# Attention halves stored apart and added at the output projection, inverse roots spread by transposes, and a new order of the attention's steps

## The chip, the core and the metric

The kernel runs on one core of a Trainium2 chip. A core has TensorE (matrix products), VectorE, ScalarE, GpSimd and SyncE, which here only issues DMAs. Each works off its own queue of instructions in order and waits on semaphores for the others. In the profile they are PE (PEld for its weight loads), DVE, ACT, POOL and SP. The metric is the device time of one execution in microseconds (us), as the median of several runs.

## The reference

Two groups of tokens, 1024 and 512, go through one encoder layer with a model width of 1024. All is f32. Cut to what matters:

```python
def _encoder_layer(x, mem, ...):
    h = _rmsnorm(x, norm_mix_g)
    dq, dk, dv, gq, gk, gv = jnp.split(h @ w_in, SPLITS, axis=-1)
    ...                                            # partial rope on dq, dk
    d_out = _diff_attention(dq, dk, dv, lam)       # 4 heads of 128, p0 - lam * p1
    d_out = _rmsnorm(d_out, diff_subln_g) * (1.0 - lambda_init)
    ...                                            # head norm and axial rope on gq, gk
    g_out = _gqa_attention(gq, gk, gv)             # 8 query heads of 64, 2 key/value heads
    x = x + jnp.concatenate([d_out, g_out], axis=-1) @ w_out
    h, m = _rmsnorm(x, norm_xattn_g), _rmsnorm(mem, norm_mem_g)
    ...                                            # cross attention, 4 heads of 256, 256 memory tokens
    h = _rmsnorm(x, norm_ffn_g)
    u = h @ w_up                                   # 1024 x 5632, then a convolution of width 3
    ...
    x = x + (jax.nn.silu(a) * b) @ w_down
    return x                                       # a last _rmsnorm follows
```

## The kernel before

Every f32 operand of a product is split into an upper and a lower part (`hi`, `lo`), and each product is made of three: hi x hi, lo x hi, hi x lo. Tokens are taken in 12 tiles of 128 (8 of the first group, 4 of the second).

The first part of the program (`trunk_phase`, until about 866 us) computes keys and values of the memory (`kv`, L838), the input projection (`proj`, L865), and the attention. The attention goes over 72 pairs of query tiles, numbered by `no`: pairs 0 to 23 belong to the four differential heads, 24 to 71 to the two groups of four query heads. For each pair TensorE computes scores (L895 to L905), ScalarE their exponentials (L1044), TensorE turns the probabilities (`turn`, L918), ScalarE and VectorE split them (`hi` L1053, `lo` L1184), and TensorE sums them into one accumulator `t_acc` in PSUM, of 128 rows by 256 queries (`mix`, L939). For a grouped-query head, rows 0 to 63 and rows 64 to 127 of the accumulator are two partial sums over different keys.

Out of the accumulator:

- Differential head: ScalarE copies it to `mixed` (`out`, L1060) and squares it. TensorE sums the squares (`sumsq`, L959), VectorE takes the mean, GpSimd the inverse root of 2 x 128 numbers (`sub_rstd`, L795) and two diagonal matrices with them (L798). TensorE multiplies these with a matrix of ones (`spread`, L966), by which each inverse root stands in all rows of its query's column, and VectorE multiplies (`finish`, L1197). SyncE stores 128 rows to `mix_scratch` in DRAM (L642).
- Grouped-query head: ScalarE copies rows 64 to 127 to `sq` (L1070), VectorE adds them to rows 0 to 63 (`merge`, L1203) once the buffer's store of two pairs before has landed, and SyncE stores 64 rows (L646). The next pair's first product into the accumulator waits for the merge (L939).

In the last part of the attention SyncE also loads w_out in eight parts (`out_load`, L654), which GpSimd splits (`out_split`, L703), and the first four tiles of `mix_scratch` (`mix_load`, L663), 512 KB each, which ScalarE and VectorE split (L1075 and the line `mix_lo`). The first products of the output projection are made at its end (`first_acc`, L951).

The second part (`rest_phase`) begins with the output projection: tile after tile in four parts (`acc`, L2202), VectorE adds x (`y`, L2744), ScalarE squares (L2437), VectorE takes the mean (L2748), GpSimd the inverse root (`rstd`, L1976), VectorE scales (`scale`, L2754), and TensorE turns the normed tile (`norm_turn`, L2217). Tiles 4 to 11 are loaded from `mix_scratch` (L1724) and split (`m_hi` L2431, `m_lo` L2738). GpSimd splits the query weights of the cross attention (L1986, L1989), and VectorE sums blocks of w_up (L2790). Cross attention and the convolutional network follow until 2366 us.

The order on each engine comes from planners. `plan` gives every step of the attention an engine, a due time, a duration and what it has to come after. `SHIFT` is a table of numbers that are added to the due times by kind of step and stage, and `PATIENCE` says for each engine how long it would rather wait for a step that is due sooner:

```python
    def put(self, engine, due, takes, kind, what, *after):
        rank = due + self.shift.get(stage_of(kind, what), {}).get(kind, 0.0) if self.shift else due
...
                    key = (max(r - free[e] - self.patience[e], 0.0), due)
                    if choice is None or key < choice[0]:
                        choice = (key, max(r, free[e]), kind)
```

`rest_plan` does the same for the second part, without such a table.

## Time and profile before

| | |
|---|---|
| time, median of 3 runs | 2368.79 us (2365.97 to 2370.07) |
| profiled execution | 2368.59 us, its span in the profile 2366.8 us |
| mean granted TensorE clock | 0.995 of full speed |
| TensorE busy | 2313.6 us, 98% |
| VectorE, GpSimd, ScalarE busy | 1780.4, 1321.2, 1147.3 us |
| DMA | 368.96 MB, mean 156 GB/s |

The busy time of an engine counts its instructions but not its semaphores and branches. A line of the timeline has the start, the duration and the instruction with output<-inputs; in brackets stands how long the engine was idle before it and what ended that. A count "x6" with a duration joins a run of equal instructions. The granted clock is the share of full speed that TensorE was given in a stretch. "DMA share" is the mean busy share of the 16 DMA engines; it can come out over 1 where packets lie over each other.

### The profile page before, as it was taken

The numbers are of one execution on the slowest core, as the hardware profiler recorded it, in microseconds if no ns is written. First come the engines' busy times: TensorE is split into PE (matmuls) and PEld (weight loads), VectorE is DVE, ScalarE is ACT, GpSimd is POOL, SyncE is SP. The second block draws the span as 40 slices with busy tenths as digits, with TensorE's granted clock in tenths as the row PEclk, the third lists the DMA queues.
The fourth block names the chain that finished last, engine by engine and source line by source line (L and its number), as shares of the span: only waits on it lengthen the run. The fifth ranks groups of instructions, "written<-read, shape, count | busy, mean of one in ns | idle before, by whom it ended". The sixth has DMA issues, their size and how long they took to land.

```text
span 2366.8 us, 34336 instructions
## 1 busy us (share of the span) xinstructions
PE 2313.6 (98%) x12096; PEld 1982.9 (84%) x12096; DVE 1780.4 (75%) x2644; ACT 1147.3 (48%) x2288; POOL 1321.2 (56%) x1522
## 2 busy tenths in 40 slices
PE   8999999999999999999999999999999999999998
PEld 7998998889998978888878888878877888888886
DVE  5447777889888967676643379988768888888888
ACT  4446665656677852123322245544444444444444
POOL 3453644688878612063150067767656666666663
PEclk9999999999999999999999999999999999999999
DMA  8853434432222049888863344333353333333332
GB/s 355 337 213 130 161 132 163 172 109 90 96 81 84 13 153 331 288 298 289 301 238 133 107 169 134 116 120 129 121 192 94 100 94 96 100 94 97 100 94 111
DMA packets 163209, 368.96 MB, mean 156 GB/s; under 512 B 16864, under 2 KB 52064, under 8 KB 152544
## 3 DMA queue, kind: packets, MB, share of 16 engines
q1 hardware_dynamic: 163040, 366.77, 45.3%
q8 instruction: 98, 1.61, 0.3%
q14 instruction: 71, 0.58, 0.1%
HBM read 284.92 MB, written 81.79 MB: 155 GB/s over the span
## 4 chain that ended last, share of the span: by engine, by line
PE 79%; DVE 8%; POOL 4%; DMA 4%; issue 3%; ACT 1%; SPq 1%; POOLq 0%; DVEq 0%; ACTq 0%
PE r_bank L2296 28%; PE r_bank L2202 10%; PE t_proj L865 9%; PE r_bank L2170 8%; PE r_bank L2235 4%; PE t_acc L939 4%; PE t_turn L918 3%; PE t_scores L838 2%; PE t_scores L895 1%; PE r_bank L2283 1%; PE r_bank L2254 1%; PE t_scores L899 1%; PE t_scores L904 1%; PE t_scores L905 1%; PE t_acc L865 1%
## 5 line engine op out<-in xcount | busy, mean ns | idle before, releaser
L865 PE MATMUL t_proj<-t_w_hi,t_hbuf 128*128 128x384 f32 x1056 | 306.2, 344 | 0.0
L2943 DVE TENSOR_TENSOR r_x_p<-r_bank,r_x_p 128x512 f32<-128x512 f32 x280 | 182.8, 682 | 48.0 <-PE r_bank L2296 47.0
L1164 DVE TENSOR_REDUCE t_max_neg<-t_scores 128x1 f32<-128x1024 f32 (+1 forms) x192 | 195.6, 1037 | 20.2 <-PE t_scores L899 17.2
L1044 ACT ACTIVATE t_prob<-t_scores,t_max_neg 128x1024 f32<-128x1024 f32 (+1 forms) x192 | 187.4, 979 | 38.6 <-DVE t_max_neg L1164 30.9
L865 PEld LDWEIGHTS t_proj<-t_w_hi,t_hbuf 128*128 128x128 f32 x1056 | 193.9, 188 | 7.3 <-issue 5.8
L1184 DVE TENSOR_TENSOR t_pt_lo<-t_turn,t_pt_hi 128x512 fp32r<-128x512 f32 x240 | 163.4, 687 | 39.9 <-ACT t_pt_hi L1053 36.7
L1053 ACT CAST t_pt_hi<-t_turn 128x512 fp32r<-128x512 f32 x240 | 139.9, 587 | 106.2 <-PE t_turn L918 84.5
L2797 DVE SCALAR_TENSOR_TENSOR r_conv<-r_rows,r_taps,r_conv 128x511 f32<-128x511 f32 (+3 forms) x134 | 157.1, 1173 | 30.2 <-ACT r_conv L2592 27.9
L865 PE MATMUL t_proj<-t_w_lo,t_hbuf 128*128 128x384 f32 x528 | 177.4, 336 | 0.0
L1976 POOL TENSOR_TENSOR r_stat<-r_stat,minus_half 128x1 f32<-128x1 f32 x24 | 16.1, 669 | 268.4 <-DVE r_stat L2748 268.4
L2044 POOL TENSOR_TENSOR r_s_lo<-r_s_raw,r_s_hi 128x512 fp32r<-128x512 f32 x87 | 128.2, 1479 | 61.7 <-ACT r_s_hi L2490 61.7
L2071 POOL TENSOR_TENSOR r_wd_lo<-r_wd_raw,r_wd_hi 128x512 fp32r<-128x512 f32 x72 | 110.7, 1538 | 79.7 <-ACT r_wd_hi L2495 79.3
L2044 POOL TENSOR_TENSOR r_w_lo<-r_w_raw,r_w_hi 128x512 fp32r<-128x512 f32 x67 | 114.8, 1715 | 72.1 <-ACT r_w_hi L2490 72.1
L918 PE MATMUL t_turn<-ident,t_prob 128*128 128x128 f32 x960 | 142.3, 274 | 3.7 <-DVE t_qk L1159 1.9
L939 PE MATMUL t_acc<-t_pt_hi,t_v_hi 128*128 128x256 f32 x480 | 139.7, 308 | 6.3 <-DVE t_mixed L1203 4.0
L2170 PE MATMUL r_bank<-r_hs_hi,r_w_hi 128*128 128x512 f32 x352 | 137.8, 391 | 4.1 <-DVE r_s_conv L2797 4.1
L2027 POOL TENSOR_TENSOR r_sd_lo<-r_sd_raw,r_sd_hi 128x512 fp32r<-128x512 f32 x74 | 109.0, 1477 | 58.8 <-ACT r_sd_hi L2504 58.6
L2170 PE MATMUL r_bank<-r_hs_hi,r_w_lo 128*128 128x512 f32 x352 | 137.5, 391 | 0.0
L2170 PE MATMUL r_bank<-r_hs_lo,r_w_hi 128*128 128x512 f32 x352 | 137.4, 390 | 0.0
L939 PE MATMUL t_acc<-t_pt_lo,t_v_hi 128*128 128x256 f32 x480 | 127.6, 282 | 0.0
L918 PEld LDWEIGHTS t_turn<-ident,t_prob 128*128 128x128 f32 x960 | 112.2, 141 | 18.1 <-issue 6.4
L2022 POOL TENSOR_TENSOR r_w_lo<-r_stage,r_w_hi 128x1024 fp32r<-128x1024 f32 x42 | 103.7, 2468 | 34.0 <-ACT r_w_hi L2485 34.0
(350 smaller groups left out, 7371.5 us busy)
## 6 DMA issues: line engine op xcount, KB each, us to landing
t_hbuf<-split_x SPq DMA_DIRECT2D x60, 1024.0 KB, 4.8
block_sums<-r_block SPq DMA_DIRECT2D x128, 256.0 KB, 3.2
r_block<-in_w_up_units SPq DMA_DIRECT2D x88, 256.0 KB, 4.7
r_stage<-in_w_up_units SPq DMA_DIRECT2D x44, 512.0 KB, 3.5
r_s_raw<-block_sums SPq DMA_DIRECT2D x87, 256.0 KB, 2.6
r_w_raw<-in_w_up_units SPq DMA_DIRECT2D x66, 256.0 KB, 2.6
split_x<-t_hbuf SPq DMA_DIRECT2D x12, 1024.0 KB, 8.7
r_block<-in_w_down SPq DMA_DIRECT2D x40, 256.0 KB, 4.5
```

What stands on the lines that cost most here:

```text
L865: ins = nc.tensor.matmul(proj_bank(i), l, r[:, k, :], start=(k == 0 and j == 0), stop=(k == KT - 1 and j == 2))
L918: ins = nc.tensor.transpose(ps_t[:, slot, kk * 2 * P + qt * P:kk * 2 * P + (qt + 1) * P], prob[:, n % PSLOTS, keys], ident[:, :])
L939: ins = nc.tensor.matmul(ps_o[:, 0:2 * P], l, r, start=(c == 0 and kk == 0 and j == 0), stop=(c == p.chunks - 1 and kk == 1 and j == len(t ...
L1044: nc.scalar.activation(prob[:, n % PSLOTS, 0:p.keys], ps_s[:, n % 2, 0:p.keys], ACT.Exp, bias=max_neg[:, n % COLS:n % COLS + 1], accum_out ...
L1164: nc.vector.tensor_reduce(max_neg[:, n % COLS:n % COLS + 1], ps_s[:, n % 2, 0:p.keys], AX.X, ALU.max, negate=True).then_inc(max_done, 1)
L1184: nc.vector.tensor_tensor(pt_lo[:, n % 2, :], ps_t[:, slot, :], f32(pt_hi[:, n % 2, :]), ALU.subtract).then_inc(ptlo_done, 1)
L2044: nc.gpsimd.tensor_tensor(wop_lo[slot][:, :], wop_raw[slot][:, :], f32(wop_hi[slot][:, :]), ALU.subtract).then_inc(op_ready, 1)
L2170: ins = nc.tensor.matmul(one_bank(s), l, r, start=(k == 0 and j == 0), stop=(k == KT - 1 and j == 2))
L2202: ins = nc.tensor.matmul(acc(t)[:, cols], l[:, k, :], r[:, cols], start=(k == 0 and j == 0), stop=(k == KT - 1 and j == 2), skip_group_che ...
L2296: ins = nc.tensor.matmul(out, l, r, start=(first and j == 0), stop=(last and j == 2), skip_group_check=onto)
L2797: return nc.vector.scalar_tensor_tensor(out, src, tap_of(j, s, i), out, ALU.mult, ALU.add)
L2943: nc.vector.tensor_tensor(x_p[:, t, cols], down_bank(q), x_p[:, t, cols], ALU.add).then_inc(p_add, 1)
```

## The change

There are three parts, and nothing else in what is computed changes.

**Halves stored apart.** `mix_scratch` has 512 more rows. For a grouped-query pair ScalarE now copies all 128 rows of the accumulator to `mixed`, as for a differential one, after the store of two pairs before has landed. SyncE stores both halves, 128 KB, to two places. `merge` is gone from VectorE. The next pair's first product waits for the copy. Where a tile is loaded for the output projection, a second DMA of 256 KB brings the other halves of the grouped-query heads into the upper-part buffer (`h_hi`), and GpSimd adds them in, 128 x 4 x 128 elements, before ScalarE's split: `mix_add` for tiles 0 to 3, `m_add` for tiles 4 to 11.

**Inverse roots.** The diagonal matrices and the product with ones are replaced by two transposes of a column of inverse roots that is read 128 times.

**Order.** `SHIFT` and `PATIENCE` have new numbers, a few due times and conditions follow the parts above, and the new GpSimd steps enter both plans. At the start all four loads of memory now come before the first load of its weights, and VectorE splits all eight parts of the memory (L1087) ahead of the first weights (L1093), where it split two, then the weights, then six. In the second part TensorE's second and fourth `norm_turn` stand one part of the projection later.

```diff
-PATIENCE = {"PE": 0.0, "DVE": 0.289, "ACT": 0.314, "POOL": 0.203, "SP": 0.0}
+PATIENCE = {"PE": 0.0, "DVE": 0.0, "ACT": 0.565, "POOL": 0.516, "SP": 0.0}
 SHIFT = {
-    "": {"axial_load": -234.355, "first_acc": 105.798, "h_load": -442.544, "key_out": -603.419, "key_store": -87.738,
+    "": {"axial_load": -1070.3, "first_acc": 971.055, "h_load": -128.363, "key_out": 128.746, "key_store": 588.333,
...
@@ plan
-            put("POOL", b + 2.0, 1.4, "sub_rstd", (p,), ("sub_mean", (p,)))
-            put("PE", b + 3.6, 0.5, "spread", (p,), ("sub_rstd", (p,)))
-            put("DVE", b + 4.4, 0.45, "finish", (p,), ("spread", (p,)))
+            put("POOL", b + 2.0, 0.7, "sub_rstd", (p,), ("sub_mean", (p,)), ("spread", (pairs[p.no - 2],)) if p.no >= 2 else None)
+            put("PE", b + 2.9, 0.22, "spread", (p,), ("sub_rstd", (p,)))
+            put("DVE", b + 3.6, 0.45, "finish", (p,), ("spread", (p,)))
...
-            put("ACT", b, 0.38, "out", (p,), ("mix", (p, p.chunks - 1)), merged, ("spread", (prev,)) if prev.diff else None)
-            put("DVE", b + 0.4, 0.42, "merge", (p,), ("out", (p,)), ("store", (pairs[p.no - 2],)))
-            put("SP", b + 1.0, 0.07, "store", (p,), ("merge", (p,)))
+            put("ACT", b, 0.38, "out", (p,), ("mix", (p, p.chunks - 1)), ("store", (pairs[p.no - 2],)))
+            put("SP", b + 0.5, 0.13, "store", (p,), ("out", (p,)))
...
-        put("ACT", pairs[-3].start + 4 * t, 1.06, "mix_hi", (t,), ("mix_load", (t,)))
+        put("POOL", pairs[-3].start + 4 * t - 1.5, 1.1, "mix_add", (t,), ("mix_load", (t,)))
+        put("ACT", pairs[-3].start + 4 * t, 1.06, "mix_hi", (t,), ("mix_add", (t,)))
@@ trunk_phase
-                        sp.wait_ge(merged, p.no - n_diff + 1)
-                        sp.dma_start(head_rows(p), mixed[0:HD, p.no % 2, :]).then_inc(mixed_stored[p.no % 2], 16)
+                        sp.wait_ge(copied, p.no + 1)
+                        sp.dma_start(head_rows(p), mixed[:, p.no % 2, :]).then_inc(mixed_stored[p.no % 2], 16)
...
+                    sp.dma_start(h_raw[0][:, :, cols], turned_mix[:, 0:KT, cols]).then_inc(tile_loaded[t % 2], 16)
+                    sp.dma_start(f32(h_hi[0][:, HK:KT, cols]), turned_mix[:, KT:KT + HK, cols]).then_inc(tile_loaded[t % 2], 16)
...
+                elif kind == "mix_add":
+                    t, = what
+                    pool.wait_ge(tile_loaded[t % 2], 32 * (t // 2 + 1))
+                    cols = slice(t * P, (t + 1) * P)
+                    raw = h_raw[0][:, HK:KT, cols]
+                    nc.gpsimd.tensor_tensor(raw, raw, f32(h_hi[0][:, HK:KT, cols]), ALU.add).then_inc(tile_added, 1)
...
-                    pool.wait_ge(sub_rstd_done, p.no + 1)
-                    for qt in range(2):
-                        nc.gpsimd.tensor_scalar(sq[:, qt * P:(qt + 1) * P], ident[:, :], sub_r[:, p.no % 2, qt:qt + 1], 1.0,
-                                                ALU.mult, ALU.mult).then_inc(sub_diag_done, 1)
...
-                    nc.tensor.matmul(ps_t[:, slot, 0:2 * P], ones[:, :], sq[:, :], start=True, stop=True).then_inc(spread_done, 1)
+                    for qt in range(2):
+                        column = sub_r[:, p.no % 2, qt:qt + 1].to_broadcast([P, P])
+                        ins = nc.tensor.transpose(ps_t[:, slot, qt * P:(qt + 1) * P], column, ident[:, :])
+                    ins.then_inc(spread_done, 1)
...
-                        nc.scalar.copy(sq[0:HD, :], ps_o[HD:P, 0:2 * P]).then_inc(copied, 1)
...
-                elif kind == "merge":
-                    p, = what
-                    dve.wait_ge(*stored_before(p))
-                    dve.wait_ge(copied, p.no + 1)
-                    nc.vector.tensor_tensor(mixed[0:HD, p.no % 2, :], ps_o[0:HD, 0:2 * P], sq[0:HD, :], ALU.add).then_inc(merged, 1)
@@ rest_plan
-            put("ACT", b - 4, 1.06, "m_hi", (t,), ("m_load", (t,)))
+            if not xo:
+                put("POOL", b - 6, 1.1, "m_add", (t,), ("m_load", (t,)))
+            put("ACT", b - 4, 1.06, "m_hi", (t,), ("m_load", (t,)) if xo else ("m_add", (t,)))
@@ rest_phase
+                    if t < NT:
+                        lows = mix_view[:, KT:KT + HK, t * P:(t + 1) * P]
+                        sp.dma_start(f32(m_tiles(t)[0][:, HK:KT, :]), lows).then_inc(m_loaded[n % 4], 16)
...
+                if kind == "m_add":
+                    t, = what
+                    n = t - EARLY
+                    pool.wait_ge(m_loaded[n % 4], m_count(n))
+                    hi, _, raw = m_tiles(t)
+                    nc.gpsimd.tensor_tensor(raw[:, HK:KT, :], raw[:, HK:KT, :], f32(hi[:, HK:KT, :]), ALU.add).then_inc(m_added, 1)
```

Line numbers in the rows of the changed kernel below are its own: L646 is L649 there, L654 is L657, L663 is L667 and L668, L1976 is L1989, L1986 and L1989 are L1999 and L2002.

SyncE's queue around the loads of w_out (`wo_raw`), before, in the second group of query heads:

```order
152 L646 DMA mix_scratch<-t_mixed 64x256 x8
153 L654 DMA wo_raw_75<-in_w_out 128x1024
154 L654 DMA wo_raw_76<-in_w_out 128x1024
155 L654 DMA wo_raw_77<-in_w_out 128x1024
156 L654 DMA wo_raw_78<-in_w_out 128x1024
157 L654 DMA wo_raw_79<-in_w_out 128x1024
158 L654 DMA wo_raw_80<-in_w_out 128x1024
159 L654 DMA wo_raw_81<-in_w_out 128x1024
160 L654 DMA wo_raw_82<-in_w_out 128x1024
161 L646 DMA mix_scratch<-t_mixed 64x256 x17
```

The same place now:

```order
142 L649 DMA mix_scratch<-t_mixed 2x64x256 x8
143 L657 DMA wo_raw_75<-in_w_out 128x1024
144 L657 DMA wo_raw_76<-in_w_out 128x1024
145 L657 DMA wo_raw_77<-in_w_out 128x1024
146 L649 DMA mix_scratch<-t_mixed 2x64x256
147 L657 DMA wo_raw_78<-in_w_out 128x1024
148 L657 DMA wo_raw_79<-in_w_out 128x1024
149 L657 DMA wo_raw_80<-in_w_out 128x1024
150 L657 DMA wo_raw_81<-in_w_out 128x1024
151 L657 DMA wo_raw_82<-in_w_out 128x1024
152 L649 DMA mix_scratch<-t_mixed 2x64x256 x16
```

One store of a pair has moved in after the third of the eight loads.

SyncE's queue at the end of the attention, where the first four tiles are loaded (`h_raw`, and now `h_hi` for the other halves), before:

```order
161 L646 DMA mix_scratch<-t_mixed 64x256 x17
162 L663 DMA h_raw_89<-mix_scratch 128x8x128 x3
163 L646 DMA mix_scratch<-t_mixed 64x256
164 L663 DMA h_raw_89<-mix_scratch 128x8x128
165 L646 DMA mix_scratch<-t_mixed 64x256 x6
```

And now, behind the same store (of pair 63):

```order
153 L667 DMA h_raw_89<-mix_scratch 128x8x128
154 L668 DMA h_hi_83<-mix_scratch 128x4x128
155 L667 DMA h_raw_89<-mix_scratch 128x8x128
156 L668 DMA h_hi_83<-mix_scratch 128x4x128
157 L667 DMA h_raw_89<-mix_scratch 128x8x128
158 L668 DMA h_hi_83<-mix_scratch 128x4x128
159 L667 DMA h_raw_89<-mix_scratch 128x8x128
160 L668 DMA h_hi_83<-mix_scratch 128x4x128
161 L649 DMA mix_scratch<-t_mixed 2x64x256 x7
```

The store of pair 64 stood behind three loads and now stands behind four tiles of two loads each.

GpSimd's queue at the start of the output projection (`r_stat` rows are inverse roots, `r_wxq` the splits of w_xq), before:

```order
720 L1976 TENSOR_TENSOR r_stat<-r_stat,minus_half 128x1 x2
721 L1986 TENSOR_SCALAR r_wxq_hi_14172<-r_wxq_raw_14176 128x512
722 L1989 TENSOR_TENSOR r_wxq_lo_14174<-r_wxq_raw_14176,r_wxq_hi_14172 128x512
...
728 L1989 TENSOR_TENSOR r_wxq_lo_14174<-r_wxq_raw_14176,r_wxq_hi_14172 128x512
729 L1976 TENSOR_TENSOR r_stat<-r_stat,minus_half 128x1 x10
```

And now:

```order
721 L1989 TENSOR_TENSOR r_stat<-r_stat,minus_half 128x1
722 L1983 TENSOR_TENSOR h_raw_90<-h_raw_90,h_hi_84 128x4x128
723 L1989 TENSOR_TENSOR r_stat<-r_stat,minus_half 128x1
724 L1999 TENSOR_SCALAR r_wxq_hi_14014<-r_wxq_raw_14018 128x512
...
733 L2002 TENSOR_TENSOR r_wxq_lo_14016<-r_wxq_raw_14018,r_wxq_hi_14014 128x512
734 L1983 TENSOR_TENSOR h_raw_90<-h_raw_90,h_hi_84 128x4x128
735 L1989 TENSOR_TENSOR r_stat<-r_stat,minus_half 128x1
736 L1983 TENSOR_TENSOR h_raw_91<-h_raw_91,h_hi_85 128x4x128 x4
737 L1989 TENSOR_TENSOR r_stat<-r_stat,minus_half 128x1 x9
```

The first addition stands ahead of the second inverse root, two more (rows 726 and 731, left out) among the four splits, the fourth ahead of the third root, and four ahead of the fourth.

## Rows read from the trace of the kernel before

**Rows 1.** The page's part 1: busy time, share and instructions of each engine.

```profile
PE 2313.6 (98%) x12096; PEld 1982.9 (84%) x12096; DVE 1780.4 (75%) x2644; ACT 1147.3 (48%) x2288; POOL 1321.2 (56%) x1522
```

**Rows 2.** TensorE's waits, whole span: line <- releaser: us, times, longest.

```profile
PE t_scores L838 <- DVE t_xkv_lo L1093: 8.7, 2, 8.5
...
PE t_acc L939 <- DVE t_mixed L1203: 4.0, 3, 1.9
PE r_bank L2217 <- DVE r_normed L2754: 3.7, 1, 3.7
...
PE t_turn L918 <- DVE t_qk L1159: 1.9, 3, 1.0
```

**Rows 3.** Windows: length, PE, PEld, DVE, ACT, POOL busy, granted clock, DMA share, GB/s.

```profile
700.00:750.00 50.00, 47.22 (x310) 42.28 (x310) 45.20 (x96) 39.54 (x90) 42.36 (x65) 1.00 0.23 68
757.60:761.00 3.40, 3.40 (x15) 3.16 (x14) 2.49 (x6) 1.58 (x3) 2.84 (x4) 0.50 0.09 19
834.80:866.00 31.20, 28.55 (x181) 24.12 (x180) 24.76 (x48) 22.11 (x48) 8.85 (x11) 1.00 0.33 93
880.00:898.00 18.00, 14.29 (x63) 11.54 (x62) 16.11 (x17) 7.44 (x9) 8.88 (x7) 0.91 1.11 341
```

**Rows 4.** Timeline of TensorE, a spread at 352.9 and two transposes at 231.2.

```profile
231.22 0.42 PE L878 MATMUL t_turn<-ident,t_nat 128*128 128x128 f32 x2
231.39 0.42 PE L865 MATMUL t_proj<-t_w_hi,t_hbuf 128*128 128x384 f32 x1
...
352.91 0.59 PE L966 MATMUL t_turn<-t_sq,t_ones 128*128 128x256 f32 x2
353.15 0.47 PE L939 MATMUL t_acc<-t_pt_hi,t_v_hi 128*128 128x256 f32 x1
```

**Rows 5.** Groups of instructions, 0 to 880 us: busy, mean ns | idle before.

```profile
L703 POOL TENSOR_TENSOR wo_lo<-wo_raw,wo_hi 128x512 fp32r<-128x512 f32 x16 | 20.6, 1289 | 1.3
...
L1203 DVE TENSOR_TENSOR t_mixed<-t_acc,t_sq 64x256 f32<-64x256 f32 x48 | 19.7, 410 | 8.7 <-ACT t_sq L1070 5.0 <-DMA mix_scratch<-t_mixed 3.5
```

**Rows 6.** Timeline at the w_out loads, SyncE and VectorE.

```profile
738.44 14.04 SPq L654 DMA_DIRECT2D wo_raw<-in_w_out  x8
...
756.75 0.42 DVE L1203 TENSOR_TENSOR t_mixed<-t_acc,t_sq 64x256 f32<-64x256 f32 x1 [2.31 <-DMA mix_scratch<-t_mixed]
```

**Rows 7.** Timeline of the start, ScalarE, VectorE and TensorE.

```profile
7.78 2.02 DVE L1093 TENSOR_TENSOR t_xkv_lo<-t_xkv_raw,t_xkv_hi 128x256 fp32r<-128x256 f32 x4
8.17 3.96 ACT L978 ACTIVATE t_mem_hi<-t_mem_raw,t_gain_cols 128x512 fp32r<-128x512 f32 x6 [1.29 <-DMA t_mem_raw<-in_mem_turned]
...
9.72 5.62 DVE L1087 SCALAR_TENSOR_TENSOR t_mem_lo<-t_mem_raw,t_gain_cols,t_mem_hi 128x512 fp32r<-128x512 f32 x6
...
27.85 0.33 PE L865 MATMUL t_proj<-t_w_hi,t_hbuf 128*128 128x384 f32 x1
```

**Rows 8.** Timeline at the end of the attention, SyncE and TensorE.

```profile
837.80 4.48 SPq L663 DMA_DIRECT2D h_raw<-mix_scratch  x3
...
847.34 0.36 PE L939 MATMUL t_acc<-t_pt_hi,t_v_hi 128*128 128x256 f32 x1 [1.14 <-DVE t_mixed L1203]
```

**Rows 9.** Timeline at the start of the output projection, four engines.

```profile
887.07 1.04 ACT L2431 CAST h_hi<-h_raw 128x1024 fp32r<-128x1024 f32 x1 [1.04 <-DMA h_raw<-mix_scratch]
...
889.62 1.09 PE L2217 MATMUL r_bank<-ident,r_normed 128*128 128x128 f32 x8 [3.71 <-DVE r_normed L2754]
...
890.73 2.13 POOL L1989 TENSOR_TENSOR r_wxq_lo<-r_wxq_raw,r_wxq_hi 128x512 fp32r<-128x512 f32 x1
...
900.71 1.29 POOL L1989 TENSOR_TENSOR r_wxq_lo<-r_wxq_raw,r_wxq_hi 128x512 fp32r<-128x512 f32 x1
...
903.23 0.55 POOL L1976 TENSOR_TENSOR r_stat<-r_stat,minus_half 128x1 f32<-128x1 f32 x1 [1.23 <-DVE r_stat L2748]
903.82 1.28 DVE L2754 SCALAR_TENSOR_TENSOR r_normed<-r_x_mo,r_stat,r_gain 128x1024 f32<-128x1024 f32 x1 [0.66 <-POOL r_stat L1976]
...
905.79 1.03 PE L2217 MATMUL r_bank<-ident,r_normed 128*128 128x128 f32 x8
```

107 lines of the change are left out of this document (55 added, 52 removed).

## The prediction

> **What bounds the kernel now.** I read the page's busy shares first, then TensorE's waits by line, then windows of single stretches with their granted clock, then the timeline at the four places that the change touches. TensorE is busy 98% of a span of 2366.8 us; VectorE has 75%, GpSimd 56% [rows 1]. So only two things count: TensorE's own work, and the few places where it runs dry. Those are short: all its waits for the merged halves make 4.0 us in three, those at the first memory projection 8.7, the one for a normed tile at the output projection 3.7 [rows 2]. A wait costs more than itself where the clock falls: after the longest wait for a merge the granted clock was 0.50 for 3.4 us, at which 3.4 us hold 1.7 us of work [rows 3] (its second line). VectorE is the engine nearest behind in the second half of the attention, 45.2 us of 50 [rows 3] (its first line). The profiled execution took 2368.59 us, 1.8 more than its span, and is 0.2 below the median of the three runs. A measurement of this kernel can tell about 0.2% from no change, that is 4.7 us.
>
> **1. Root spread by transposes.** Before, one product with the matrix of ones stands in two records, and the next instruction starts 0.24 us after the first of them (352.91 to 353.15). Two transposes of 128x128 let the next start after 0.17 (231.22 to 231.39) [rows 4]. There are 24 pairs of differential heads, so 24 x -0.07 = -1.7 us, in a stretch in which TensorE is hardly ever idle: I take **-2**. GpSimd loses 48 instructions that it makes the diagonal with, on no path that waits. The Trainium skill speaks against this edit ("TensorE: Matmul & The Clock Gate", Part 4: PE-mode transpose): a 128x128 transpose takes some 275 ns in a kernel, most of it the access of SBUF. The records do last 0.27 (0.42 for two, the second 0.15 later), but their starts lie closer than that; what the sum would be if they did not overlap is a rival below.
>
> **2. The w_out loads and the merge that is gone.** Before, SyncE issues eight loads in a row, which hold it 14.04 us from 738.44, and the store that stands behind them keeps VectorE's merge waiting for 2.31 us (756.75) [rows 6]. That gives two of the three merge waits (4.0 less the last, 1.1, is 2.9) [rows 2, 8], and the half clock, 1.7 [rows 3]: 4.6 us. Now a store stands after the third load, five loads then hold the next store, and there is no merge on VectorE: 48 x 0.41 = 19.7 us of it go [rows 5]. Of the small waits for t_qk (1.9 in three [rows 2]), which come from a VectorE that is 90% busy, I take 1.4 as gained. **-6**; from -2 (five of eight loads still hold SyncE 14.04 x 5/8 = 8.8 us, and now it is ScalarE's copy that waits behind the store) to -8.
>
> **3. Startup.** TensorE's first product waits for VectorE until 8.5 [rows 2]. Before, VectorE splits two parts of the memory, then the first weights in four quarters (2.02 us from 7.78), then six more parts from 9.72 on. Now all eight parts stand ahead of the weights. ScalarE ends the eighth upper part at 8.17 + 3.96 = 12.1; the lower part behind it takes 0.94 (5.62 / 6), and the first quarter of the weights 0.5 [rows 7]: TensorE starts at about 13.6 to 14, 5 to 5.5 later. What it then does runs without the waits that it had: three parts of the projection took from 8.54 to 27.85, 19.3 us [rows 7], and at the pitch of its instructions they are 17.1, so 14 + 17.1 = 31.1, 3.3 behind. I take off 1.3 for waits of the same kind (the memory's norm) soon after: **+2**, from 0 to +4.
>
> **4. End of the attention.** Before, SyncE issues three tile loads of 512 KB in 4.48 us from 837.80, then the store whose landing the merge awaits; behind the merge, 0.42 long, TensorE goes on at 847.34, having lost 1.14 [rows 8], so the store landed at about 846.8. Now all four tiles are loaded ahead of this store, each by two DMAs (512 and 256 KB): 3 MB instead of 1.5, where a third load waits for the first to land, a fourth for the second. Before, the third was issued when the first had landed, some 4 us after the start; now that takes about 6 and the fourth's turn 8, and the store lands behind the traffic: 846.8 becomes some 851. ScalarE's copy of the accumulator waits for it (the exponentials of the next pairs and the casts of turned probabilities stand behind it on that queue), and the next product into the accumulator waits for the copy. So a wait of 1.1 becomes one of 5 to 6, at which the clock falls (1.7 more): +6. TensorE was idle 31.20 - 28.55 = 2.65 us in this stretch [rows 3] (its third line) and waited there for other things too; those are covered by the long wait, and the merge's 0.42 behind each copy is gone: **+3**, from 0 (the store waits no longer than today) to +6.
>
> **5. Start of the output projection.** GpSimd's queue was: two inverse roots, four splits of w_xq (each two instructions; from 889.8, 0.9 ahead of the subtraction at 890.73, to 900.71 + 1.29 = 902.0, 12.2 us), then the third root at 903.23; the norm scaled with it ended at 903.82 + 1.28 = 905.1 and TensorE turned it at 905.79, with no wait [rows 9]. The slack is 0.7 us. Now four additions of halves stand in this queue ahead of the third root. No row shows such an addition; the nearest is a subtraction of the same size, 128x512, by GpSimd: 1.29 at the median [rows 5], and at this place 1.29 to 2.13 [rows 9]. The first addition is ahead of the second root and waits for the second DMA of its tile: the tile alone came at 887.07, so about 888.5, ending at 890.2; the root 0.9, the norm 1.3, and TensorE goes on at about 892.9, having done one part of the projection more (2.7 us): +0.6 against 889.62. The splits begin at 891.1 instead of 889.8, and three additions come among them: 891.1 + 12.2 + 3 x 1.29 (to 2.13) = 907.2 to 909.7 for the third root, 909.7 to 912 for TensorE, which arrives at 905.8 + 0.6 = 906.4: a wait of 3.3 to 5.6. With the half clock, 1.7, this is +0.6 + 3.3 + 1.7 = **+5.5**, up to +8. Down to 0: if the tile's halves land early and GpSimd's other waits for the w_xq weights move into the gaps. DMA is at 341 GB/s and a share of 1.11 in this stretch [rows 3] (its fourth line), and 2 MB more go through it, so I stay away from that end. The additions for tiles 8 to 11 stand ahead of the fourth root, which TensorE needs only four parts later. Four of the twelve additions are in the attention, on a GpSimd that had little to do there: 8.85 us of 31.2 [rows 3]; nothing.
>
> **6. The new order of the rest of the attention.** Every step up to 850 us stands a little elsewhere. No row prices it. TensorE's small waits there are single ones of up to 1.9 [rows 2]; three more or three fewer are 5 us: **0**, from -5 to +5.
>
> Sum: -2 - 6 + 2 + 3 + 5.5 + 0 = +2.5, so 2368.6 + 2.5 = 2371.1 for the profiled execution, and with 0.2 to the median 2371.3: I say **2371**.
>
> **Rivals.** (1) *The adds are hidden*: at the output projection the halves arrive early and at the end of the attention the store goes through between loads, so that terms 4 and 5 are nothing: 2368.8 - 2 - 6 + 2 = 2362.8. For it: GpSimd idled 1.23 us ahead of the third root, and the first root of this stretch is long done. Against: a slack of 0.7 for three additions. (2) *GpSimd and VectorE slow each other down all through the stretch*, the case on the slow side: all four additions ahead of the third root take 2.13, and so do all four subtractions of the splits, of which before two were at that and two at 1.29 [rows 9] (two of them shown). The first root comes 0.84 later than in term 5, the third at 909.7 + 0.84 + 2 x 0.84 = 912.2, TensorE turns its norm at 914.7 where it could at 907.2: 0.6 + 0.84 + 7.5 + 1.7 = 10.6 in place of 5.5, and the additions for tiles 8 to 11, 8.5 us, hold the fourth root by about one more: 2371.3 + 6 = 2377. For it: VectorE is busy 16.11 of 18 us there [rows 3]. By the Trainium skill ("GPSIMD Engine Reference", 1. Specifications) the two share their SBUF interfaces when VectorE has two SBUF inputs, as the sums of weight blocks there have. Decided by the third root: past 909.4 the time is on the slow side. (3) *Transposes do not overlap*: each then holds TensorE for the 0.27 that its record lasts, 2 x 0.27 - 0.24 = +0.30 in place of -0.07, 24 times: +7.2 for -2, 2371.3 + 9.2 = 2380.5. By the section of the skill named above the same (2 x 0.275) comes out; the rows speak against it [rows 4]. But the operand is now one column read 128 times, which no row shows. (4) *Nothing changes*: waits only move, 2369.
>
> **How the numbers follow.** Forecast 48%, (1) 29%, (2) 13%, (3) 5%, (4) 5%. Taken alone the forecast holds 2366 to 2375: of its 48, 4 are faster by over 0.2% (below 2364.1), 33 within, 11 slower (above 2373.5). Of (1) 23 are faster, 6 within; (2) 12 slower, 1 within; (3) 5 slower; (4) 5 within. So 27% faster, 45% within, 28% slower. The range is 2362 to 2378: terms 2, 4, 5 and 6 leave about 3, 3, 4 and 5 us on either side, 7.7 together if they are independent; it takes in (1), the edge of (2), and leaves out (3).
>
> **What would show it.** Startup: the first product at 13.6 or later, not 8.5. Spread: the pitch from the first transpose to the next instruction, 0.17 or 0.54. Around 738 to 761: SyncE's store between the loads, no half clock after it. End of the attention: the landing of the first store behind the tile loads, and a wait of ScalarE's copy until 851. Output projection: duration of an addition (1.3 or 2.1), the third root later than 906.5, a wait of TensorE for a normed tile of over 3 us with a half clock after it; none at the fourth. I am wrong if TensorE waits there no more than today, or if the new order in between gains or loses over 5 us by small waits.

## The result

The changed kernel takes 2379.48 us (median of 6 runs, 2372.95 to 2384.35), the kernel before 2366.22 over its 6. The ratio is 1.0057, with a 95% interval of 1.0044 to 1.007: slower by 0.57%, some 13 us. The prediction was 2371, with 2362 to 2378: the direction of its sum was right, its size a fifth, and the range missed the time.

The profiled execution took 2380.86 us, its span is 2379.0. The page's part 1, then TensorE's waits over the whole span (us, times, longest), both of the changed kernel:

```profile
PE 2306.8 (97%) x12096; PEld 1978.7 (83%) x12096; DVE 1768.8 (74%) x2596; ACT 1143.7 (48%) x2288; POOL 1322.1 (56%) x1486
```

```profile
PE t_scores L847 <- DVE t_xkv_lo L1097: 12.4, 1, 12.4
PE r_bank L2230 <- DVE r_normed L2770: 11.4, 4, 5.6
PE t_acc L946 <- ACT t_mixed L1069: 10.4, 2, 8.9
```

TensorE is busy 6.8 us less than before [rows 1], and the span is 12.2 longer. All three waits of [rows 2] that the prediction rested on are there again and longer: 12.4 for 8.7, 11.4 for 3.7, 10.4 for 4.0.

Where the time goes is best read by comparing the start of the same instruction of TensorE in two traces. The table has, for points in the program named by their time in the kernel before, how much later (+) or earlier (-) than there TensorE comes to them. 144 is the last projection of the memory, 755 and 828 are turned probabilities (all differential heads are done by then), 866 the last product of the attention, 929 the fifth normed tile, 2334 the last group of products. The last column is the ratio of times, with its interval, against the kernel before on the same chip; the rows come from different chips, so two rows are compared by their ratios and not by their medians (0.001 is 2.4 us). Single traces differ by a few us between 1000 and 2334 for no cause that was found, so the points up to 929 are for the mechanism and the ratio is for the worth. The one trace of the kernel before is of an execution 2.4 us above its median. In twelve of the thirteen rows the column 929 is 1 to 5 us more favourable than the ratio, so differences between rows are safer than a row's own distance to the kernel before.

| kernel | 144 | 755 | 828 | 866 | 929 | 2334 | median us | ratio |
|---|---|---|---|---|---|---|---|---|
| changed | +2.1 | -6.6 | -8.7 | +1.1 | +11.6 | +12.3 | 2379.5 | 1.0057 (1.0044 to 1.007) |
| e1_two_stores | +2.0 | -6.7 | -8.9 | -2.2 | +5.7 | +4.3 | 2375.6 | 1.0039 (1.0024 to 1.0054) |
| e2_no_adds | +2.7 | -6.0 | -8.2 | +1.8 | +3.5 | +4.4 | 2372.8 | 1.0028 (1.0018 to 1.0038) |
| e3_old_order | -0.4 | +1.2 | +6.4 | +12.2 | +21.9 | +21.2 | 2389.9 | 1.0096 (1.0079 to 1.0113) |
| e4_roots_only | -0.3 | -7.3 | -9.2 | -10.1 | -10.9 | -14.3 | 2358.6 | 0.9974 (0.9962 to 0.9987) |
| e5_store_first | +2.2 | -6.7 | -8.8 | -5.8 | +1.7 | +7.6 | 2368.0 | 1.0014 (1.0004 to 1.0023) |
| e6_no_pool_add | +2.1 | -6.6 | -8.4 | +1.2 | +8.6 | +6.9 | 2377.1 | 1.0047 (1.0032 to 1.0061) |
| e7_merge_new_order | +1.6 | +2.6 | +4.6 | +8.4 | +10.0 | +12.3 | 2378.4 | 1.0053 (1.004 to 1.0067) |
| e8_roots_ahead | +2.2 | -6.2 | -8.2 | -5.4 | -2.2 | -2.2 | 2365.6 | 1.0001 (0.9989 to 1.0013) |
| e9_old_order_two_stores | -0.3 | -0.4 | +1.9 | +2.8 | +9.1 | +10.1 | 2379.0 | 1.0047 (1.0028 to 1.0066) |
| e10_old_start | +3.4 | -5.4 | -7.6 | -7.9 | -5.0 | -4.9 | 2363.7 | 0.9994 (0.9983 to 1.0006) |
| e11_diagonal_kept | +0.2 | -3.4 | -2.9 | -3.6 | -3.1 | -1.1 | 2361.4 | 0.9983 (0.997 to 0.9996) |
| e12_roots_store_first | -0.2 | -7.2 | -7.2 | -8.0 | -8.7 | -15.7 | 2356.6 | 0.998 (0.9968 to 0.9993) |

So the changed kernel is 8.7 us ahead at 828, and loses 9.8 to the end of the attention and 10.5 more up to the fifth normed tile.

**End of the attention.** The chain of waits, two links of it:

```profile
834.68 6.46 DMA h_hi<-mix_scratch
...
842.18 6.30 DMA mix_scratch<-t_mixed
```

The timeline of the same place, ScalarE and TensorE:

```profile
848.57 0.37 ACT L1069 COPY t_mixed<-t_acc 128x256 f32<-128x256 f32 x1 [8.26 <-DMA mix_scratch<-t_mixed]
...
849.08 0.55 PE L946 MATMUL t_acc<-t_pt_hi,t_v_hi 128*128 128x256 f32 x1 [8.88 <-ACT t_mixed L1069]
```

And a window over the end of this wait, columns as in [rows 3]:

```profile
848.00:853.00 5.00, 3.92 (x13) 3.53 (x14) 1.71 (x4) 3.42 (x9) 0.69 (x1) 0.50 0.13 46
```

SyncE comes to the store at 842.18, after the fourth tile's loads, which waited for the second's to land (834.68 + 6.46). The store lands 6.30 later, the copy has then waited 8.26 and TensorE 8.88, where it waited 1.14 [rows 8]; the granted clock is 0.50 from 843.4, inside the wait, to 853.6, so TensorE works at it for 4.6 us; before, the clock did not fall at this place. By this the loss of 9.8 is accounted for: 7.7 of longer wait and some 2.3 of half clock.

**Start of the output projection.** The last store of the attention and what stands behind it, from the chain of waits:

```profile
868.19 9.80 DMA mix_scratch<-t_mixed
878.23 0.18 POOLq L1582
```

It landed 9.80 us after its issue; GpSimd clears the semaphores of the first part behind it (L1582), and SyncE goes on with the second part's loads only after that, at 880.05. Before, the same load came at 873.86. Then GpSimd and TensorE in the timeline:

```profile
893.50 1.64 POOL L1983 TENSOR_TENSOR h_raw<-h_raw,h_hi 128x512 f32<-128x512 f32 x1 [12.78 <-DMA h_hi<-mix_scratch]
...
896.22 1.22 POOL L1999 TENSOR_SCALAR r_wxq_hi<-r_wxq_raw 128x512 fp32r<-128x512 f32 x1 [0.58 <-DMA r_wxq_raw<-in_w_xq_heads]
897.02 1.97 PE L2230 MATMUL r_bank<-ident,r_normed 128*128 128x128 f32 x8 [5.58 <-DVE r_normed L2770]
899.07 2.25 POOL L1983 TENSOR_TENSOR h_raw<-h_raw,h_hi 128x512 f32<-128x512 f32 x1
...
909.41 2.26 POOL L1983 TENSOR_TENSOR h_raw<-h_raw,h_hi 128x512 f32<-128x512 f32 x1
911.64 0.54 POOL L1989 TENSOR_TENSOR r_stat<-r_stat,minus_half 128x1 f32<-128x1 f32 x1
...
914.55 1.47 PE L2230 MATMUL r_bank<-ident,r_normed 128*128 128x128 f32 x8 [3.41 <-DVE r_normed L2770]
```

These answer to [rows 9]. The first addition waits 12.78 us for its second load, and the second root (895.10) stands behind it: 5.58 us of wait for 3.71. The third root is at 911.64 for 903.23. The same four splits of w_xq stand ahead of it, which now begin at 896.22 and not at 889.81, because these weights are loaded behind the late store too, and three additions of 1.29 to 2.26 stand among them: 3.41 of wait for none. The half clock after the second wait lasts for 4.4 us of work, until 901.4; before it was 3.4 [rows 3]. Counted without the part of the projection that the new order moves ahead, TensorE falls 3.6 us back up to the second normed tile, 4.1 more up to the third and 2.8 more up to the fifth: this is the 10.5.

### The profile page after: what moved, and what is told of

Its sections match the earlier page's. It is cut to its first block, busy times and chain, and to the rows that moved or that the text cites. A ratio compares the mean times of both kernels' runs of the same rounds, so it can differ in the third digit from the quotient of the medians.

```text
span 2379.0 us, 34238 instructions
## 1 busy us (share of the span) xinstructions
PE 2306.8 (97%) x12096; PEld 1978.7 (83%) x12096; DVE 1768.8 (74%) x2596; ACT 1143.7 (48%) x2288; POOL 1322.1 (56%) x1486
## 4 chain that ended last, share of the span: by engine, by line
PE 76%; DVE 10%; POOL 5%; DMA 4%; issue 2%; ACT 1%; SPq 1%; POOLq 0%; DVEq 0%; ACTq 0%
PE r_bank L2309 26%; PE t_proj L874 9%; PE r_bank L2215 9%; PE r_bank L2183 6%; PE r_bank L2248 4%; PE t_acc L946 4%; PE t_scores L847 4%; PE t_turn L927 3%; POOL t_w_lo L698 1%; DVE r_x_s L2834 1%; PE t_scores L913 1%; DMA mix_scratch<-t_mixed 1%; PE t_scores L914 1%; PE t_scores L904 1%; PE t_acc L874 1%
## 5 line engine op out<-in xcount | busy, mean ns | idle before, releaser
L1989 POOL TENSOR_TENSOR r_stat<-r_stat,minus_half 128x1 f32<-128x1 f32 x24 | 15.2, 635 | 254.7 <-DVE r_stat L2764 228.3
L946 PE MATMUL t_acc<-t_pt_hi,t_v_hi 128*128 128x256 f32 x480 | 137.5, 303 | 11.8 <-ACT t_mixed L1069 10.4
L927 PEld LDWEIGHTS t_turn<-ident,t_prob 128*128 128x128 f32 x960 | 111.0, 141 | 21.2 <-issue 12.9
```

Of the source, the lines that this page charges most:

```text
L927: ins = nc.tensor.transpose(ps_t[:, slot, kk * 2 * P + qt * P:kk * 2 * P + (qt + 1) * P], prob[:, n % PSLOTS, keys], ident[:, :])
L946: ins = nc.tensor.matmul(ps_o[:, 0:2 * P], l, r, start=(c == 0 and kk == 0 and j == 0), stop=(c == p.chunks - 1 and kk == 1 and j == len(t ...
```

## The experiments

### The store of two halves

```diff
-                        sp.dma_start(head_rows(p), mixed[:, p.no % 2, :]).then_inc(mixed_stored[p.no % 2], 16)
+                        for z in range(2):
+                            sp.dma_start(head_rows(p, z), mixed[z * HD:(z + 1) * HD, p.no % 2, :]).then_inc(mixed_stored[p.no % 2], 16)
```

> The changed kernel, but each grouped-query pair is stored by two DMAs of 64 rows instead of one of 2x64 rows. Theory A (the store of two halves moves on few DMA engines: in the changed kernel's trace its mean share over the 16 engines is one tenth for 3.5 us, and the last one of the attention takes 9.80 us to land against 4.87 before): each store lands in about 2 us as before, the last one in about 5, the one behind the tile loads in about 4.5 instead of 6.3, so the memory loads of the second part begin 4 to 5 us sooner and the kernel takes 5 to 7 us less than the changed one, about 2373. Rival B (the stores land late because of the traffic around them): nothing moves, 2379. Rival C (the second store's issue, 0.45 us each on SyncE, holds up others): 0 to 3 us slower than the changed kernel.

Measured: 2375.6, and the loss at the end of the attention is 6.7 for 9.8, that after it 7.9 for 10.5. Theory A holds, at 4 us instead of the 5 to 7 expected: the last store lands 6.2 after its issue and not 5, the one behind the tile loads after 3.7. The intervals of the two ratios overlap, so it is the landings that decide. How the bytes move is seen in a quiet stretch of 12 us, cut in 40 slices of 0.3 us, with the busy share of the 16 DMA engines in tenths and the rate; the changed kernel first (two stores of 128 KB, the second starting at slice 18, counted from 0):

```profile
DMA  0001101211111000001011111111400000000000
GB/s 0 0 20 41 48 24 24 58 31 41 48 48 48 27 34 0 0 0 27 34 48 27 41 24 44 48 51 48 99 0 0 0 0 0 0 0 0 0 0 7
```

and with two DMAs of 64 rows each per pair:

```profile
DMA  0000000045360000000000006354000000000100
GB/s 0 0 0 0 0 0 0 0 106 113 89 157 0 27 0 0 0 0 0 0 0 0 0 0 147 72 119 99 0 0 0 0 0 0 0 0 0 55 0 0
```

The same 128 KB take 3.2 to 3.5 us, some 40 GB/s, and a share of a tenth to two of the engines, or 1.2 us at around 115 GB/s and three to six tenths. The list of DMA issues of the second kernel has the landings (KB each, median us), of the half stores and of the differential heads' stores of 128 rows:

```profile
mix_scratch<-t_mixed SPq DMA_DIRECT2D x96, 64.0 KB, 2.1
...
mix_scratch<-t_mixed SPq DMA_DIRECT2D x24, 128.0 KB, 1.7
```

So it is not the 128 KB: with 128 rows in one stride they land in 1.7 us. No landing time stands in the list for the stores of 2x64 rows. It is the form "2x64x256" that stood in the order's rows. The Trainium skill says so ("DMA: Bandwidth & Descriptors", Rules for kernel authors): an outermost dimension of a size below 16 confines the DMA to at most so many engines. By that rule this store has two of sixteen, and the share of a tenth to two agrees.

### Old order, new structure

```diff
-PATIENCE, SHIFT of the changed kernel
+PATIENCE, SHIFT of the kernel before
```

> The changed kernel with the table of shifts and the patience of the kernel before (halves and transposes as changed). The changed trace gains some 10 us between the start and 830 us, before the losses. If the new order gives these: 5 to 8 us slower than the changed kernel in that stretch, so 2385. If they come from the merge that is gone and the transposes: as fast as the changed kernel in that stretch within 3 us, and 2 us sooner at the first projections, where the order of the memory's splits is the old one again. The end of the attention depends on where the old numbers put the tile loads among the stores.

Measured: 2389.9, slower than the changed kernel by 10, and at 828 us 15 later than it (+6.4 for -8.7), with 13.1 us of waits for ScalarE's copies in three. The same with two stores per pair:

> The changed kernel with the old table of shifts and patience and with two stores per grouped-query pair. With the old table and one store of 2x64 rows the kernel took 2390, 31 us more than the transposes alone with the same table, and TensorE waited 13.1 us for copies behind stores. If the slow store makes these: the three waits mostly go and the kernel comes to 2372 to 2376 (what is left being the end of the attention and the output projection). If the halves cost as much in the old order whatever the store: 2385 or more.

Measured: 2379.0, so 11 of the 31 us between this structure and the transposes alone come from the form of the store. Not as much as I expected: at 828 it is +1.9, where the transposes alone are at -9.2. So with the old table the new structure costs 11 us in the attention with two stores and 15.6 with one, and the new table takes most of that back (-8.9 at the same point). That the halves cost these 11 is not shown: counted by TensorE's 3500th instruction, at 578 us before, the two traces are 5.8 apart already (-1.4 for -7.2). The first half is stored only after it, and what waits were added up to there are mostly for VectorE's splits. The plan's due times and conditions changed for other steps as well, and the old numbers were made for the old ones. The new order is a repair of the new structure more than a gain of its own.

To try it with the merge kept, VectorE's merges were put into the new order at the planned time of the copy plus 0.46:

```diff
+    merges = [(begin + 0.46, "merge", what) for begin, kind, what in order["ACT"] if kind == "out" and not what[0].diff]
+    order["DVE"] = sorted(order["DVE"] + merges, key=lambda s: s[0])
```

> The kernel before with transposes and with the new order of the attention, but with VectorE's merge as before (put into VectorE's order 0.46 after its copy in the plan) and no additions at the output projection. If the new order is worth something by itself: ahead of the transposes alone by 2 to 4 us at 830 us in spite of a start that is 2 us late, 2356. If it only repairs what the stored halves cost: equal or behind, 2359 to 2364. The end of the attention: tile loads of 512 KB each now all ahead of the store of pair 64, so a wait for the merge of some 3 us.

Measured: 2378.4, worse than either guess, with TensorE waiting 11.9 us for merges in 22 places. That shows that this order has no room for merges; since the places of the merges were mine and not the planner's, it does not settle what the order is worth by itself.

### Transposes alone

```diff
-                    nc.tensor.matmul(ps_t[:, slot, 0:2 * P], ones[:, :], sq[:, :], start=True, stop=True).then_inc(spread_done, 1)
+                    for qt in range(2):
+                        column = sub_r[:, p.no % 2, qt:qt + 1].to_broadcast([P, P])
+                        ins = nc.tensor.transpose(ps_t[:, slot, qt * P:(qt + 1) * P], column, ident[:, :])
+                    ins.then_inc(spread_done, 1)
```

> The kernel before with the roots spread by two transposes of a column read 128 times, and nothing else. My term: -2 us (-0.07 each for 24), 2364. Rival (the transposes do not overlap, 0.27 each): +7. In the trace: the next instruction 0.14 to 0.17 us after the first transpose, or 0.5.

Measured: 0.9974, -6 us, over three times my term, and clear of no change. The timeline of one spread:

```profile
350.25 0.38 PE L966 MATMUL t_turn<-ident,t_sub_r 128*128 128x128 f32 x2
350.39 0.36 PE L937 MATMUL t_acc<-t_pt_hi,t_v_hi 128*128 128x256 f32 x1
350.59 0.28 PE L937 MATMUL t_acc<-t_pt_lo,t_v_hi 128*128 128x256 f32 x1
```

The two transposes start 0.14 ahead of the next instruction, and that one is 0.20 long, so from 350.25 to 350.59 it is 0.34 us. In [rows 4] the same lines are 352.91, 353.15 and then 353.45: 0.54. I had taken the first difference alone, 0.24 against 0.17 of two other transposes, and the second record of the product was still under way behind it. To part TensorE's work from the chain, the diagonal matrices were still made, and waited for, though nothing read them:

```diff
+                    pool.wait_ge(sub_rstd_done, p.no + 1)
+                    for qt in range(2):
+                        nc.gpsimd.tensor_scalar(sq[:, qt * P:(qt + 1) * P], ident[:, :], sub_r[:, p.no % 2, qt:qt + 1], 1.0,
+                                                ALU.mult, ALU.mult).then_inc(sub_diag_done, 1)
```

> The kernel before with the transposes, while GpSimd still makes the two diagonal matrices (which nothing reads now) and TensorE still waits for them. The transposes alone gave -6.6 us (7.3 in the trace by 565 us). Theory A (TensorE's own work: records of the spread take 2 x 0.38 before and 2 x 0.27 now, 0.21 per pair, 5.0 in all): about -5 remains. Theory B (the chain from mean to spread is shorter by 0.8 us and it is this that TensorE stops waiting for): -1 to -2 remains.

Measured: 0.9983, and -3.4 at 755 in the trace where the transposes alone have -7.3. The ratios do not tell the two kernels apart (0.997 to 0.9996 and 0.9962 to 0.9987), the traces do. The starts of all 24 spreads give TensorE's own share: from the first record to the second instruction behind the spread it is 0.61 us in the mean before, 0.39 in both kernels with transposes, so 0.22 per pair and 5.4 in all. What parts the two is idle time: from 190 us to the point 755 TensorE idles 9.2 us before, 7.7 with the transposes alone and 10.4 with the diagonal kept. So some three quarters of the 7.3 are TensorE's own work, as theory A had it, and the rest are small waits that the shorter chain takes away, with 18.7 us of GpSimd, which I had costed at nothing. The kept diagonal does not price that chain cleanly: GpSimd makes it there and, unlike before the change, also waits for the spread of two pairs before.

### End of the attention

```diff
+    order["SP"] = move(order["SP"], [("store", 64)], ("mix_load", 0))
+    order["SP"] = move(order["SP"], [("store", 65)], ("mix_load", 1))
```

> The changed kernel with two stores per grouped-query pair, and in SyncE's order the stores of pairs 64 and 65 taken from behind the four tile loads to behind the first and the second of them. With two stores alone TensorE still waits 5.7 us for ScalarE's copy at the end of the attention and falls from 7.8 ahead of the kernel before to 1.6 ahead. Theory (the store waits its turn on SyncE and its bytes wait behind those of the loads): that wait goes to under 1.5 us and the fall from 6.2 to about 1; the kernel takes 4 to 6 us less than with two stores alone, 2370. Rival (the copy waits for the loads' traffic whatever the place of the store): the wait stays at 4 to 6, 2375.

Measured: 2368.0, less than with two stores alone by 5.9 us by the ratios (7.6 by the medians). TensorE's wait for the copy there is gone, the longest wait left in the stretch is one of 2.1 for a split, and the loss is 3.0 for 6.7. Of the 9.8 us of the changed kernel, 3.1 are the form of the store, 3.7 its place behind 3 MB of loads, 3.0 remain. The store of pair 65 was moved as well, so 3.7 is for both.

### Start of the output projection

Second loads and additions of tiles 4 to 11 left out:

```diff
-                        sp.dma_start(f32(m_tiles(t)[0][:, HK:KT, :]), lows).then_inc(m_loaded[n % 4], 16)
-                    nc.gpsimd.tensor_tensor(raw[:, HK:KT, :], raw[:, HK:KT, :], f32(hi[:, HK:KT, :]), ALU.add).then_inc(m_added, 1)
```

> The changed kernel without the second load of tiles 4 to 11 and without GpSimd's eight additions in the output projection (so the second halves are missing from the output); orders and stores as in the changed kernel. Theory A: of the 10.4 us that TensorE falls behind from the end of the attention to the fourth normed tile (1.1 to 11.5 us behind the kernel before), about 5 come from the late landing of the last store and stay, and about 5 come from loads and additions and go: 2374 to 2375. Rival B (the additions and their loads are all of it): 2369. Rival D (they hide behind the late start): 2379.

Measured: 2372.8 and a loss of 1.7 in place of 10.5. Loads and additions are nearly all of it in this stretch; the late last store makes TensorE lose almost nothing where the rest is not late too (theory A was wrong there). Only the additions left out:

> The changed kernel without GpSimd's eight additions in the output projection (the second halves of tiles 4 to 11 are loaded but not added, so they are missing from the output). Between the end of the attention and the fourth normed tile the changed kernel falls 10.5 us behind the one before, and 1.6 us without loads and additions. If GpSimd's time makes it (three additions of 1.3 to 2.3 ahead of the third root): 3 to 5 us behind, most of it at the second and first turned tile. If the second loads make it (2 MB more, and SyncE's queue): 7 to 9.

Measured: 2377.1, a loss of 7.4: the additions are 3.1 of the 10.5, the second loads 5.7, by the wider of the two guesses. By the ratio the additions are 2.4 us, which their intervals do not tell from nothing. The parting also goes by what is taken out first, since the waits lie over each other: without the additions all that the loads cost comes at the fourth tile, where the changed kernel itself loses 2.8. The loads alone taken out were not run. Why loads cost that much is seen on ScalarE and GpSimd of this kernel:

```profile
916.58 1.05 ACT L2441 CAST h_hi<-h_raw 128x1024 fp32r<-128x1024 f32 x1 [2.26 <-DMA h_hi<-mix_scratch]
...
922.60 0.55 POOL L1986 TENSOR_TENSOR r_stat<-r_stat,minus_half 128x1 f32<-128x1 f32 x1 [15.58 <-DVE r_stat L2758]
```

ScalarE's queue has the splits of tiles 8 to 11 ahead of the third normed tile's split (917.53) and the next square. They now wait for a tile each, 2.26 us for the last, and the fourth root follows at 922.60; TensorE waits 4.07 for it. In SyncE's queue the sixteen DMAs of tiles 4 to 11 (and two others) are issued from 884.68 to 911.4; before, the eight (and the same two) took from 879.58 to 897.5.

Additions and splits that are not needed yet taken behind the roots, squares and norms, on top of the stores in order:

```diff
+    order["POOL"] = move(order["POOL"], [("m_add", 4)], ("rstd", 1))
+    order["POOL"] = move(order["POOL"], [("m_add", t) for t in (5, 6, 7)], ("rstd", 2))
+    order["POOL"] = move(order["POOL"], [("m_add", t) for t in (8, 9, 10, 11)], ("rstd", 3))
+    order["ACT"] = move(order["ACT"], [("m_hi", t) for t in (5, 6, 7)], ("square", 2))
...
+    order["DVE"] = move(order["DVE"], [("m_lo", t) for t in (8, 9, 10, 11)], ("scale", 3))
```

> As the run with the stores of pairs 64 and 65 between the loads, and at the output projection each addition that is not needed yet is taken behind the inverse root it stands in front of: on GpSimd the first behind the second root, three behind the third, four behind the fourth; ScalarE's and VectorE's splits of the same tiles likewise. Theory (the roots wait in GpSimd's queue behind additions): the waits of TensorE for normed tiles fall from 9.6 us to about 4, as before, and the 7.9 us lost there to under 2; 6 us less than without: 2364. Rival (VectorE and the loads are as late, so that the projection itself waits for split tiles): half of it, 2367 to 2370.

Measured: 2365.6, a loss of 3.2 for the 7.5 of e5, and 3.1 us less than e5 by the ratios, whose intervals overlap. The third and fourth normed tiles are turned without a wait (900.41, 912.20 in its trace), and in place of it TensorE waits 3.04 once later, at 927.17. That is for the fifth normed tile and not, as the rival had it, for a split one: VectorE's splits of tiles 8 to 11, 7.92 us from 911.30, now stand ahead of its sums for this norm. By the ratio it is level with the kernel before.

### Start

```diff
+    order["SP"] = move(order["SP"], [("mem_load", k) for k in (1, 2, 3)], ("xkv_load", 0))
+    order["DVE"] = move(order["DVE"], [("mem_lo", k) for k in range(2, KT)], ("xkv_lo", 0))
```

> As the run with roots ahead (two stores, stores 64 and 65 among the tile loads, roots ahead of the additions), with the start of the kernel before: first weights loaded behind the first part of the memory, VectorE splits two parts of the memory, the weights, then six parts. My term for the start: +2 for the new one, so 2363 to 2364 here, and the milestone of TensorE at 144 us 0 instead of 2.2 behind. Rival: made up later by waits, no difference, 2365.6.

Measured: 0.9994, whose interval takes in the ratio of e8. TensorE starts at 8.6 again and is +3.4 at 144 all the same: it ends a wait for another engine at 41.49, and the granted clock is 0.50 for 3.4 us from 42.6.

```profile
41.49 0.35 PE L865 MATMUL t_scores<-t_xkv_hi,t_mem_hi 128*128 128x256 f32 x1 [2.91 <-ACT t_value_res L1034]
```

Up to 37 us it is level with the kernel before (+0.1), where the changed kernel is 3.8 behind. This wait and its half clock, some 4.6 us together, which the changed kernel does not have, then take that away. So the run shows the cost of the late start up to there, but not what an early start is worth without the new wait. Why ScalarE is late at 41.49 is not settled.

### A better kernel

The transposes alone beat both kernels. With the store of pair 64 behind the first tile load, and ScalarE's squares no longer waiting for the spread:

> The kernel before with the transposes alone, and two small things more: the store of pair 64 behind the first tile load instead of behind the third, and ScalarE's squares wait for the sums of squares and not for the spread, since the spread no longer reads that buffer. The transposes alone gave 2358.6 against 2365.3. The wait for the merge behind the tile loads (1.1 us before) should go: 2357 to 2358, which the measurement can hardly tell from 2358.6. Rival (the first tiles land later and the first products of the output projection wait): 2359 to 2361.

Measured: 0.998 (0.9968 to 0.9993), 2356.6 where the kernel before had 2362.3 on the same chip. That is as good as the transposes alone and not better; the two small things are worth nothing that can be measured. The 1.1 us of wait for the merge that the moved store was to take away is not in the trace of the transposes alone either.

## Why the prediction was wrong

The forecast was +2.5 us against the kernel before and the measured change +13.3. Two terms were far too small, 4 by 6.8 and 5 by 5.0, and in both the first step that failed is the landing of a store, which was taken from the old store of 64 rows. Term 1 gained more than forecast and term 2 less, which offset each other in part.

**Term 1, transposes: -2, measured -6.** Direction right, size wrong. The step that failed is the pitch, -0.07 per pair where all 24 spreads give -0.22: one difference of starts was read in front of an instruction that begins while the product's second record is not through. The rival that the transposes do not overlap is refuted. What the Trainium skill gives for one ("TensorE: Matmul & The Clock Gate", Part 4), some 275 ns, is how long the record lasts here too, but not what it costs: the instruction behind both starts 0.14 after the first. "On no path that waits" for GpSimd's diagonal was wrong too: some quarter of the gain in the trace.

**Term 2, w_out loads: -6, measured -3.5 with term 6, or less.** Right in the mechanism, too large in the sum. The wait behind the loads became one of 1.6 for ScalarE's copy, and the half clock after it is gone. With terms 1 and the start taken out, the changed kernel gains 3.5 by 828 from terms 2 and 6 together (-8.7 + 7.3 - 2.1). The transposes alone gain 1.9 more between 755 and 828, as no half clock came after the wait for the merge in that one trace: in e12, of the same order there, it came (751.6) and nothing was gained. By e4's own -9.2 the rest would be 1.6 and not 3.5. The 1.4 for the small waits for t_qk was not there: they are 1.4 in two now, for 1.9 in three.

**Term 3, start: +2, measured +2.1** at 144, TensorE starting at 12.4 and not 13.6. The size holds, and the mechanism as far as it can be read: up to 37 us TensorE is 3.8 behind, where I had worked out 3.3, and of the 1.7 that it then makes up 0.8 is the wait for the memory's norm (L865 for ScalarE's L997), which is gone. Where the rest comes from is not settled.

**Term 4, end of the attention: +3, measured +9.8.** The mechanism was the one described: the copy behind a store behind the tile loads, then the half clock. Two steps failed. The landing of the store was taken as before, "846.8 becomes some 851", that is 13 us after the first tile load; it came 15.4 after it (833.07 to 848.5), because the store itself was slow. With two stores it came 13.5 after (831.62 to 845.1), and TensorE waited 5.71, inside the 5 to 6 of the forecast. And I took 3 us off for waits that the long one would cover and for the merge: with two stores the loss is still 6.7, all of the longer wait (4.6) and of the half clock, which cost 2.3 and not 1.7.

**Term 5, start of the output projection: +5.5, measured +10.5.** Three steps failed. The second load of the first tile was to land at 888.5 and the splits of w_xq to begin at 891.1; they did at 893.5 and 896.22, since the last store landed late and SyncE's loads stand behind it. With two stores they came as forecast, at 887.62 and 890.33, and 2.6 us were won. From the start of the splits to the third root it took 15.4 us in both kernels, a little less than the 16.1 to 18.6 of the forecast, so the queue of GpSimd was priced well. Then, I priced the additions alone, with 5.5, and by e6 they are 3.1. I had 2 MB of further loads in hand, said that they would keep the term off its low end, and gave them no price; by e2 and e6 they are 5.7 of the 10.5. Last, the fourth tile was to cost nothing, and costs 2.8 in the changed kernel: 0.9 of wait, and a second half clock of 1.7 after the wait for the third. "The fourth root, which TensorE needs only four parts later" left out that ScalarE's splits of tiles 8 to 11 stand ahead of the square that this root needs.

**Term 6, the order: 0.** What the old table does in the new structure (15 later at 828, 11 with two stores) lay outside my bounds of 5 either way; I had asked what the new order does to the old kernel, while it was made for the new one.

**What was missed altogether** is the form of the store. It stood in the order's rows as 2x64x256 and in the changed kernel as `mix_halves[:, top:top + HD, ...]`, and I read it as 128 KB instead of 64. Its landing of 6.3 and 9.8 us is in terms 4 and 5: two stores give 3.1 and 2.6 us back there, and 4 us of the time. Rival 2 (2377, additions slow all through) was nearest in time, and its sign, a third root past 909.4, came true (911.64), but not by its mechanism: of the four additions up to this root two took 1.3 and 1.6 us and two 2.3, the long ones beside splits of VectorE with two SBUF inputs (from 897.90 and 908.60), and with two stores the root is at 905.74.

Not tried, and so open: whether the second loads cost by SyncE's queue (26.7 us of issuing for 17.9) or by the DMA engines, whose share is over 1 in this stretch before and after.

## What to carry to other kernels

A store that gets a further dimension in front is a different DMA: look at the outermost size of the row in the order before taking its landing from the trace of the old form. When a change puts loads into a stretch where DMA is full, price them by who stands behind them in the in-order queues of the engines that split or copy them, not only by the engine that does the new arithmetic. And of a change with several parts, the part that is worth having can be the one that looks smallest: here the transposes give 6 us, and the halves stored apart, with the order made for them, cost all that and 13 more.

## What the runs showed of the hardware

A store of 2x64 rows of 1 KB runs at some 40 GB/s, at a share of one to two tenths of the DMA engines; as two DMAs of 64 rows it runs at around 115; and a store of 128 rows with the same bytes lands in 1.7 us. A transpose of one column read 128 times is as quick as one of a full tile: two of them let the next instruction start after 0.14 us (up to 0.22 in some of the 24 places, by what follows), where two of full tiles let it after 0.17 [rows 4]. In the waits of 8.9 and of 5.6 us the granted clock fell to 0.50 (1.2 of 2.4 GHz) before they ended, and TensorE then worked at it for 4.6 and 4.4 us; after the wait of 1.9 it did for 3.4 [rows 2, 3].
